# A two-layer encoder trunk on one core: hi-hi and hi-lo products as one step of 512 columns

## The reference, cut

```python
# layer 0: x += even_token_mixer(...);      x += cross-attention(0);  x += swiglu(rms_norm(x))
# layer 1: x += diff_attention_mixer(...);  x += cross-attention(1);  x += top-2-of-8 experts(rms_norm(x))
def memory_cross_attention(h, mem_n, wq, wkv, wo):
    q = (h @ wq).reshape(B, L, XA_HEADS, XA_HD)
    k, v = split_cols(mem_n @ wkv, (D, D))
    ...
def swiglu(h, w_gate, w_up, w_down):            # w_gate, w_up: 1024 x 2816
    return (jax.nn.silu(h @ w_gate) * (h @ w_up)) @ w_down
```

## Time and profile before

| | |
|---|---|
| median of 3 runs | 1638.72 us (1638.66 to 1639.1) |
| the profiled execution | 1638.37 us, of which the span is 1636.5 |
| TensorE busy | 1613.6 us, 99% |
| VectorE busy | 1269.9 us, 78% |
| ScalarE busy | 1036.3 us, 63% |
| GpSimd busy | 59.7 us, 4% |
| DMA | 474.72 MB, mean 290 GB/s |
| granted TensorE clock | 0.998 of full |

### The profile page before, as it was taken

One profiled execution on the slowest core, in us unless ns is written; L12 is line 12 of the kernel. 1 busy time (PEld: TensorE's weight loads), 2 busy tenths in 40 slices (PEclk: granted clock), 3 DMA queues, 4 the chain that ended last, 5 costly groups with the idle time before them and its releaser, 6 DMA issues.

```text
span 1636.5 us, 22669 instructions
## 1 busy us (share of the span) xinstructions
PE 1613.6 (99%) x8508; PEld 1377.7 (84%) x8508; DVE 1269.9 (78%) x1070; ACT 1036.3 (63%) x908; POOL 59.7 (4%) x54
## 2 busy tenths in 40 slices
PE   7999999999999999999999999999999999999997
PEld 6998989998887798888888888888888888888886
DVE  7776646454567765798888888888888888888897
ACT  5443445544356544677777777777777777777775
POOL 1000000000000101100000000000000000000100
PEclk9999999999999999999999999999999999999999
DMA  9644435555554354799999999999979999999993
GB/s 363 199 155 155 159 125 180 180 180 193 169 184 151 129 211 168 291 357 388 370 389 374 377 386 371 374 392 366 387 290 364 376 379 364 398 380 370 403 406 151
DMA packets 226031, 474.72 MB, mean 290 GB/s; under 512 B 7698, under 2 KB 52964, under 8 KB 225972
## 3 DMA queue, kind: packets, MB, share of 16 engines
q1 hardware_dynamic: 221552, 459.01, 76.7%
q0 software_dynamic: 3104, 10.66, 1.9%
q10 hardware_dynamic: 1316, 4.24, 0.6%
HBM read 466.01 MB, written 7.87 MB: 290 GB/s over the span
## 4 chain that ended last, share of the span: by engine, by line
PE 93%; DVE 4%; ACT 1%; issue 1%; POOL 0%; DMA 0%; POOLq 0%; ACTq 0%; SPq 0%; DVEq 0%
PE ps L2329 37%; PE ps L2352 18%; PE ps L1861 15%; PE ps L1827 9%; PE ps L1847 4%; PE ps L2090 4%; DVE w_lo L395 2%; PE ps L2337 1%; ACT w_hi L391 1%; PE ps L2002 1%; PE ps L2022 1%; PE ps L2116 0%; PE ps L1956 0%; PE ps L2317 0%; DMA const<-in_consts 0%
## 5 line engine op out<-in xcount | busy, mean ns | idle before, releaser
L395 DVE TENSOR_TENSOR w_lo<-raw,w_hi 128x2048 fp32r<-128x2048 f32 x430 | 980.2, 2291 | 223.2 <-ACT w_hi L391 221.8
L391 ACT ACTIVATE w_hi<-raw 128x2048 fp32r<-128x2048 f32 x430 | 823.7, 1918 | 295.7 <-PE ps L2329 110.0
L2329 PE MATMUL ps<-w_hi,e_hi 128*128 128x512 f32 x896 | 355.2, 396 | 0.7 <-DVE w_lo L395 0.5
L2329 PE MATMUL ps<-w_hi,e_lo 128*128 128x512 f32 x896 | 349.6, 390 | 0.0
L2329 PE MATMUL ps<-w_lo,e_hi 128*128 128x512 f32 x896 | 349.0, 389 | 0.0
L2329 PEld LDWEIGHTS ps<-w_hi,e_hi 128*128 128x128 f32 x896 | 168.2, 188 | 38.0 <-DVE w_lo L395 2.6
L2329 PEld LDWEIGHTS ps<-w_hi,e_lo 128*128 128x128 f32 x896 | 168.2, 188 | 36.0
L2329 PEld LDWEIGHTS ps<-w_lo,e_hi 128*128 128x128 f32 x896 | 168.4, 188 | 33.3
L2352 PE MATMUL ps<-w_hi,at_hi 128*128 128x512 f32 x448 | 176.1, 393 | 0.1
L2352 PE MATMUL ps<-w_hi,at_lo 128*128 128x512 f32 x448 | 174.6, 390 | 0.0
L2352 PE MATMUL ps<-w_lo,at_hi 128*128 128x512 f32 x448 | 174.3, 389 | 0.0
(11 more groups left out here) (362 smaller groups left out, 1719.3 us busy)
## 6 DMA issues: line engine op xcount, KB each, us to landing
raw<-in_moe_w_up SPq DMA_DIRECT2D x112, 1024.0 KB, 7.5
raw<-in_moe_w_gate SPq DMA_DIRECT2D x110, 1024.0 KB, 7.4
raw<-in_moe_w_down SPq DMA_DIRECT2D x110, 1024.0 KB, 7.1
raw<-in_xa_wkv SPq DMA_DIRECT2D x16, 1024.0 KB, 5.0
raw<-in_ev_w_in SPq DMA_DIRECT2D x14, 1024.0 KB, 7.9
raw<-in_od_w_in SPq DMA_DIRECT2D x12, 1024.0 KB, 5.0
raw<-in_ffd_w_gate SPq DMA_DIRECT2D x11, 1024.0 KB, 5.0
raw<-in_ffd_w_up SPq DMA_DIRECT2D x11, 1024.0 KB, 5.0
```

Of the source, the lines that this page charges most:

```text
L391: nc.scalar.activation(w_hi[:, n % CUT, :], at_, ACT.Copy).then_inc(hi_cut, 1)
L395: nc.vector.tensor_tensor(w_lo[:, n % CUT, :], place(n, r, behind)[0], w_hi[:, n % CUT, :].bitcast(F32), ALU.subtract).then_inc(lo_cut, 1)
L2329: mm = T.matmul(ps[:, bank, :], s, m, start=(h == 0 and k == 0 and j == 0), stop=(h == 1 and k == 3 and j == 2))
```

## The change

`a_hi` and `a_lo` become the two halves of one tile `a_hl`, and so do `m_hi` and `m_lo`. In `wide_slab`, which takes the place of `fm_slab` for k0, q0, k1a, k1b, q1, gate and up (38 slabs; evc keeps `fm_slab`), hi times hi and hi times lo are one matmul: the stationary operand is the rounded weight piece, the moving one is 256 columns of hi and 256 of lo, and they go into two halves of one bank. The third product, lo weight times hi activation, is added to the first half. A half slab now takes a whole bank, and whoever reads it adds the two halves: `wide` is a reduction on VectorE of two banks, 1024 elements, to 512. `BANKS` and `room` count two banks for such a slab.

In gate and up a pair takes four banks, and there are two sets of them: TensorE waits for the product of the pair before last (`f_mul`). VectorE reduces gate into `f_sig` between its two `cut_lo`, raises the new semaphore `f_gate`, and after the second `cut_lo` reduces up into `f_act`; ScalarE's Silu waits for `f_gate` and works in place in SBUF; the product takes both operands from SBUF. The loops are written out as eleven pairs on all three engines.

```diff
+WIDE = ("k0", "q0", "k1a", "k1b", "q1")
-        _n += _k
+        _n += 2 * _k if _name in WIDE else _k
...
-        a_hi = sb("a_hi", [P, KT, 256], F32R)
-        a_lo = sb("a_lo", [P, KT, 256], F32R)
+        a_hl = sb("a_hl", [P, 2, KT, 256], F32R)
+        a_hi, a_lo = a_hl[:, 0, :, :], a_hl[:, 1, :, :]
...
 # ScalarE
-            def ff_pair(j, r, f):
-                cut_hi(act, g + 2 * j + AHEAD, r)
-                act.wait_ge(slab_used, g + 2 * j + 1 + 6 * r)
-                nc.scalar.activation(f_sig, ps[:, 2 * (j % 3), :], ACT.Silu).then_inc(f_silu, 1)
-                cut_hi(act, g + 2 * j + 1 + AHEAD, r)
+            def ff_pair(f):
+                cut_hi(act, g + 2 * f + AHEAD)
+                act.wait_ge(f_gate, f + 1)
+                nc.scalar.activation(f_sig, f_sig, ACT.Silu).then_inc(f_silu, 1)
+                cut_hi(act, g + 2 * f + 1 + AHEAD)
                 act.wait_ge(f_mul, f + 1)
...
 # VectorE
+            def wide(dst, b):
+                return V.tensor_reduce(dst, ps[:, b:b + 2, :].rearrange("p o (h n) -> p o n h", h=2), AX.X, ALU.add)
...
-                    freed(V.tensor_copy(dst[:, o:o + 2, :], acc(name, i, 1)), 1)
+                    freed(wide(dst[:, o:o + 2, :], (BANKS[name] + 2 * i) % 4), 2)
...
-                    freed(V.tensor_copy(xq[:, 2 * k:2 * k + 2, :], acc(f"q{i}", k, 1)), 1)
+                    freed(wide(xq[:, 2 * k:2 * k + 2, :], (BANKS[f"q{i}"] + 2 * k) % 4), 2)
...
-                cut_lo(dve, g + 2 * j + AHEAD, r)
-                cut_lo(dve, g + 2 * j + 1 + AHEAD, r)
-                dve.wait_ge(slab_used, g + 2 * j + 2 + 6 * r)
+                b = 4 * (f % 2)
+                cut_lo(dve, g + 2 * f + AHEAD)
+                dve.wait_ge(slab_used, g + 2 * f + 1)
+                wide(f_sig.rearrange("p (a n) -> p a n", a=2), b).then_inc(f_gate, 1)
+                cut_lo(dve, g + 2 * f + 1 + AHEAD)
+                dve.wait_ge(slab_used, g + 2 * f + 2)
+                link(wide(f_act.rearrange("p (a n) -> p a n", a=2), b + 2))
                 dve.wait_ge(f_silu, f + 1)
-                V.tensor_tensor(f_act, ps[:, 2 * (j % 3) + 1, :], f_sig, ALU.mult).then_inc(f_mul, 1)
+                V.tensor_tensor(f_act, f_act, f_sig, ALU.mult).then_inc(f_mul, 1)
...
 # TensorE
+            def wide_slab(n, b, hl, base=None):
+                slab_ready(n)
+                wh, wl = (shaped(w[:, n % CUT, :], KT) for w in (w_hi, w_lo))
+                for o in range(2):
+                    for k in range(KT):
+                        if base is not None and o == 0:
+                            pe.wait_ge(t_lo, base + k + 1)
+                        s_hi, s_lo = (w[:, k, o * P:(o + 1) * P] for w in (wh, wl))
+                        for j in (0, 1) if k == 0 else (1, 0):
+                            if j == 0:
+                                mm = T.matmul(pair(b + o), s_hi, hl[:, :, k, :], start=(k == 0), stop=(k == KT - 1),
+                                              skip_group_check=True)
+                            else:
+                                T.matmul(pair(b + o)[:, 0, :], s_lo, hl[:, 0, k, :], start=False, stop=False,
+                                         skip_group_check=True)
+                mm.then_inc(slab_used, 1)
...
-                    pe.wait_ge(f_low, f - 2)
+            def ff_pair(f):
+                if f >= 2:
+                    pe.wait_ge(f_mul, f - 1)
+                b = 4 * (f % 2)
+                wide_slab(g + 2 * f, b, a_hl, TURNS["ffn"][0] if f == 0 else None)
+                wide_slab(g + 2 * f + 1, b + 2, a_hl)
+            for f in range(11):
+                ff_pair(f)
+            pe.wait_ge(f_mul, 10)
```

More of the change, by code:

```diff
@@ L217, in trunk_kernel @@
             held_m = sb("held_m", [P, 2, 2048], F32, s)
-        m_hi = sb("m_hi", [P, KT, 256], F32R)
-        m_lo = sb("m_lo", [P, KT, 256], F32R)
+        m_hl = sb("m_hl", [P, 2, KT, 256], F32R)
+        m_hi, m_lo = m_hl[:, 0, :, :], m_hl[:, 1, :, :]
         hits = sb("hits", [1, 3 * NE])
@@ L291, in trunk_kernel @@
         f_silu, f_mul, f_rnd, f_low, f_add = (sem(n) for n in ("f_silu", "f_mul", "f_rnd", "f_low", "f_add"))
+        f_gate = sem("f_gate")
         oq_ps, oq_t = sem("oq_ps"), sem("oq_t")
@@ L729, in _ @@
             g = FIRST["fgu"]
-            def ff_pair(j, r, f):
-                cut_hi(act, g + 2 * j + AHEAD, r)
-                act.wait_ge(slab_used, g + 2 * j + 1 + 6 * r)
-                nc.scalar.activation(f_sig, ps[:, 2 * (j % 3), :], ACT.Silu).then_inc(f_silu, 1)
-                cut_hi(act, g + 2 * j + 1 + AHEAD, r)
+            def ff_pair(f):
[3 more added lines that the diff above has]
+                cut_hi(act, g + 2 * f + 1 + AHEAD)
                 act.wait_ge(f_mul, f + 1)
-                nc.scalar.activation(f_hi[:, bass.ds(2 * f, 2), :], f_act.rearrange("p (a n) -> p a n", a=2),
+                nc.scalar.activation(f_hi[:, 2 * f:2 * f + 2, :], f_act.rearrange("p (a n) -> p a n", a=2),
                                      ACT.Copy).then_inc(f_rnd, 1)
[L741 to L745, removed]
+            for f in range(11):
+                ff_pair(f)
             stage("fdn", 11)
@@ L1288, in _ @@
             g = FIRST["fgu"]
-            def ff_pair(j, r, f):
-                cut_lo(dve, g + 2 * j + AHEAD, r)
-                cut_lo(dve, g + 2 * j + 1 + AHEAD, r)
-                dve.wait_ge(slab_used, g + 2 * j + 2 + 6 * r)
+            def ff_pair(f):
[6 more added lines that the diff above has]
+                link(wide(f_act.rearrange("p (a n) -> p a n", a=2), b + 2))
                 dve.wait_ge(f_silu, f + 1)
-                V.tensor_tensor(f_act, ps[:, 2 * (j % 3) + 1, :], f_sig, ALU.mult).then_inc(f_mul, 1)
+                V.tensor_tensor(f_act, f_act, f_sig, ALU.mult).then_inc(f_mul, 1)
                 dve.wait_ge(f_rnd, f + 1)
-                V.tensor_tensor(f_lo[:, bass.ds(2 * f, 2), :], f_act.rearrange("p (a n) -> p a n", a=2),
-                                f_hi[:, bass.ds(2 * f, 2), :].bitcast(F32), ALU.subtract).then_inc(f_low, 1)
+                V.tensor_tensor(f_lo[:, 2 * f:2 * f + 2, :], f_act.rearrange("p (a n) -> p a n", a=2),
+                                f_hi[:, 2 * f:2 * f + 2, :].bitcast(F32), ALU.subtract).then_inc(f_low, 1)
                 dve.wait_ge(f_low, f + 1)
[L1301 to L1305, removed]
+            for f in range(11):
+                ff_pair(f)
             def fd_event():
@@ L1863, in fm_slab, with gemm_f @@
                 mm.then_inc(slab_used, 1)
-            def gemm_f(name, count, hi, lo, base=None):
+            def wide_slab(n, b, hl, base=None):
[14 more added lines that the diff above has]
+                mm.then_inc(slab_used, 1)
+            def gemm_f(name, count, hi, lo):
                 for i in range(count):
@@ L1868, in gemm_f, with gemm_w @@
                     room(name, c + 1)
-                    fm_slab(FIRST[name] + i, 0, c % 4, hi, lo, base if i == 0 else None)
+                    fm_slab(FIRST[name] + i, 0, c % 4, hi, lo)
+            def gemm_w(name, count, hl):
+                for i in range(count):
+                    c = BANKS[name] + 2 * i
+                    room(name, c + 2)
+                    wide_slab(FIRST[name] + i, c % 4, hl)
             def turn(name, src, after):
@@ L1933, in k0_slab @@
             def k0_slab(i):
-                c = BANKS["k0"] + i
-                room("k0", c + 1)
-                fm_slab(FIRST["k0"] + i, 0, c % 4, m_hi, m_lo)
+                c = BANKS["k0"] + 2 * i
+                room("k0", c + 2)
+                wide_slab(FIRST["k0"] + i, c % 4, m_hl)
             def ret_scores(h):
@@ L1991, in q_slab @@
                 def q_slab(k):
-                    c = BANKS[f"q{i}"] + k
-                    room(f"q{i}", c + 1)
-                    fm_slab(FIRST[f"q{i}"] + k, 0, c % 4, a_hi, a_lo, TURNS[name][0] if k == 0 else None)
+                    c = BANKS[f"q{i}"] + 2 * k
+                    room(f"q{i}", c + 2)
+                    wide_slab(FIRST[f"q{i}"] + k, c % 4, a_hl, TURNS[name][0] if k == 0 else None)
                 def scores(h):
-                    pe.wait_ge(acc_free, BANKS[f"q{i}"] + h + 1)
+                    pe.wait_ge(acc_free, BANKS[f"q{i}"] + 2 * h + 2)
                     if h >= 2:
@@ L2057, in _ @@
             cross(0, xa_q0, xa_k0, xa_v0, xa_pt0)
-            gemm_f("k1a", 2, m_hi, m_lo)
+            gemm_w("k1a", 2, m_hl)
             turn("ffn", tat, NORMS["ffn"] + 1)
@@ L2063, in _, with ff_pair @@
             g = FIRST["fgu"]
-            def ff_pair(j, r, f, first=False):
-                if not first:
-                    pe.wait_ge(f_low, f - 2)
[L2068 to L2078, removed]
+            def ff_pair(f):
+                if f >= 2:
[3 more added lines that the diff above has]
+                wide_slab(g + 2 * f + 1, b + 2, a_hl)
+            for f in range(11):
+                ff_pair(f)
+            pe.wait_ge(f_mul, 10)
             for i in range(11):
```

(2 more changed lines are left out.)

## The result

The changed kernel takes 1645.09 us, median of 6 runs (1645.03 to 1645.58), against 1638.97 for the kernel before (6 runs, 1638.66 to 1639.7): 1.0039 of it, 95% interval 1.0029 to 1.0050. It is 6.1 us slower; 6.2 were forecast. The profiled executions differ by 7.2 us (spans 1636.5 and 1643.7): the one of before took 1638.37 us, less than all its timed runs, the one of after 1645.58, the longest of its own.

What follows compares the result with a forecast made beforehand. TensorE was taken to bound the kernel before, a VectorE-ScalarE ring gate and up after; -0.85 (k0) -0.75 (q0) +7.5 (feed-forward) +1.07 (k1b) -0.75 (q1) = +6.2 us, 1644.9 us, range 1637.5 to 1651.5.

Steps and rivals of the forecast that it cites:

- The sum: Whole kernel: -0.85 (k0) -0.75 (q0) +7.5 (k1a, gate, up, down) +1.07 (k1b) -0.75 (q1) = +6.2 us.
- rival C: VectorE's strided read of two banks runs at half rate, 2.29 us a reduction; about 1671 us in all; chance 0.08.
- Part 3: Order in gate and up: from pair 5 TensorE waits for VectorE's w_lo; the down product ends 7.5 us later.
- the ring: Closed chain of VectorE and ScalarE operations in gate and up, 12.66 us per pair against TensorE's 11.09; chance 0.72.
- Part 1: TensorE's steps in 38 changed slabs: 5.547 us instead of 5.76, 0.213 less each, 8.1 us if TensorE stays the bound.
- rival D: TensorE's step in two pieces costs 0.240 us, so changed slabs save nothing: +8.6 us, 1647.3; chance 0.10.
- Part 4: Slabs outside gate and up: k0 -0.85, q0 -0.75, q1 -0.75, k1a -0.08, k1b +1.07 us; longer reads in k0, q0, q1 hidden.
- Rival B: In gate and up VectorE and ScalarE work neighbouring pairs side by side, TensorE stays the bound: -5.9 us, 1632.8; chance 0.10.

## Why the prediction was right, point by point

**The sum.** The mechanism and its place were right; that 6.1 us meets 6.2 so closely is in part luck. By the traces the stretches that the change touches add up to +6.9 us (7.2 less the load's 0.3), and the forecast is 0.7 short of that: 0.5 us too much gained in k0, q0 and q1 and 0.3 too little lost in gate, up and down, less 0.1 for k1a. The timed runs say 6.1 because the profiled execution of before is 0.6 under its median and the one of after 0.5 over.

**The bound and the prices of rows.** Reading the step price from starts, not from durations, was right, and so was the reduction: 22 of them in gate and up at a mean of 1218 ns, to the nanosecond the row for maxima (rows 5):

```profile
L1055 DVE TENSOR_REDUCE ta<-ps 128x512 f32<-128x1024 f32 x22 | 26.8, 1218 | 0.6 <-PE ps L1880 0.6
```

Reading n and n+256 in turn costs nothing over reading in order. That settles rival C, and with it what the Trainium skill says of lines of 8 bytes and patterns that aren't contiguous (PSUM — Partial Sum Buffer, Specifications): it speaks of matmuls, and a VectorE reduction doesn't follow it here.

**Part 3, the ring.** Forecast 12.66 us a turn, measured 12.67, and TensorE first waits at pair 5, as forecast; the excess over TensorE's pair is 1.48 us, not 1.57, because the pair is 11.19 and not 11.09. Link by link in the pieces above: Silu to `cut_hi` 0.54 (0.53 forecast), `cut_hi` to `cut_lo` 1.93 (1.94) and 2.00 (2.01), `cut_lo` to reduction 2.21 (2.20), reduction to product 1.26 (1.26), product to rounding 0.72 (0.73). From the start of gate and up to the end of the down product 194.83 us; the forecast, 447.1 less 252.6, is 194.5. The three waits ahead of the first down slabs came too: the record has 2.2 us of idle time, and by the starts (384.51, 390.44 and 397.16, where a slab takes 5.44) the second is 0.5 and the third 1.3, where 0.5 and 1.2 were forecast. The third slab starts at 397.16, where 398.15 was forecast from a start that lies 1.0 us later.

**Part 1, the step.** This is the term that was mis-sized: a slab saves 0.17 us, not 0.213, since the step in two halves takes 0.230, within the bounds of 0.2267 and 0.240 but not at the end that was taken. It shows where TensorE is the bound: four slabs of k0, q0 and q1 gained 0.61, 0.63 and 0.59 us instead of 0.85, 0.75 and 0.75. In gate and up it was invisible under the ring, as rival D had it for its own larger price. 10 ns more a step would have been D.

**Part 4, what was called hidden.** The stretches k0, q0 and q1 lost nothing else: VectorE's longer reads and the wait for a pair of banks lie in its idle time. k1b came out at 1.06 of 1.07, k1a at -0.17 where -0.08 was forecast. VectorE is free for `a_lo` at 250.96 after the subtraction at 244.29, 6.67 us; the sum of 2.20, 1.14, 2.20 and 1.22 is 6.76, and the last link is 1.13: the write of `a_lo` starts 0.09 us before the recorded end of the reduction (249.83 and 1.22).

**Rival B** needed the two engines to work side by side. Moving one line makes them do so, and then its time is nearly reached: 1634.2 against the 1632.8 that it gave. It was wrong of the kernel as written, and right of what the two engines can do.

**A slip in the range.** Its upper end was put at D with reductions of 1.3 us, "1651". By the prediction's own terms that is 1649.2: 1647.3, and 0.08 us more for each of 22 reductions in the ring and two in k1b. Nothing in the result hangs on it.

## What to carry to other kernels

Where two engines hand work to each other several times in one pass of a loop, add up the links of the closed chain, start to start, and compare it with the pass of the engine that bounds: busy shares don't show it, since VectorE with 8.4 us of work in a pair of 11.09 stood in a ring of 12.66. An operation that waits for another engine belongs behind the work that its own engine could do without that wait; here one `cut_hi` moved ahead of the wait turned 6 us lost into 4.6 gained, and a late read of k1b made it 6.1 (1632.8 us, 0.9963 of before, 0.9949 to 0.9977), the fastest of the orders that were tried, with 1632.6 for the contiguous layout no different.

And a lead hides a slow ring for a while: 0.4 us a pair over eleven pairs showed no wait of TensorE, and 1.48 us a pair cost 10.9 in all (1645.09 less 1634.18, the order without the ring) and not 16.

## What the runs showed of the hardware

A sum of pairs that lie 1 KB apart in PSUM takes as long on VectorE as a maximum of elements in order (1218 ns for 1024 elements in both, with 512 and 4 results). A matmul of 512 columns that moves activations against a fresh 128 x 128 piece of weights takes 0.230 us in a stream and one of 256 columns 0.119, where the token-major down product shows 0.2267; with the moving operand in one piece, or the lengths in another order, a pair keeps its 11.17 to 11.19 us. A VectorE instruction whose input doesn't come from the one before starts 0.08 to 0.09 us ahead of that one's recorded end (2.21 us after a subtraction of 2.29), and this has to be counted in a chain of starts.
